# A decoder trunk on one core: the 16-row tail units of v, k and ckv computed in four column groups, the RMS scaling moved into the turning product, and the norm's weights moved into the split of w_in

## What is computed

```
u = rmsnorm(h, g_attn)             # h: (528, 1024), mean over 1024
proj = u @ w_in                    # w_in: (1024, 2216)
fq, fk, fv, ff, cq, ckv, kr = split(proj)   # 512, 512, 512, 8, 384, 256, 32 columns
rmsnorm(x, g) = x * rsqrt(mean(x * x) + 1e-6) * g
```

## Time and profile before

| | |
|---|---|
| median of 3 runs | 689.05 us (688.73 to 690.02) |
| the profiled execution | 692.33 us, of it 690.6 us in the profile's span |
| PE busy | 593.6 us, 86% of the span |
| DVE, ACT, POOL busy | 235.6, 207.3, 159.5 us |
| instructions | 8906 |
| input projection, first dense product to last | 27.8 to 157.2 us from the start of the span |

### The profile page before, as it was taken

The page is one execution under the profiler, slowest core; times in us unless marked ns, Lnnn a source line. Parts: engine busy times, 40 slices in busy tenths (PEclk is TensorE's granted clock), DMA queues, the critical chain, the costliest instruction groups (busy, mean ns, idle before and its releaser), DMA issues.

```text
span 690.6 us, 8906 instructions
## 1 busy us (share of the span) xinstructions
PE 593.6 (86%) x3367; PEld 382.0 (55%) x3367; DVE 235.6 (34%) x514; ACT 207.3 (30%) x377; POOL 159.5 (23%) x232
## 2 busy tenths in 40 slices
PE   3699999998999797999899976999998788887840
PEld 3598678895665454666455543555554455454520
DVE  4653323224456566364345540111111111011105
ACT  5533223242544343453344431121211111111110
POOL 8100001110134921242300021223232222122110
PEclk9999899999999999899999976999999999999985
DMA  8900000007600001000391076999999999999929
GB/s 246 387 28 1 1 0 1 1 1 228 284 1 0 0 1 62 0 1 1 135 416 58 32 254 216 375 382 394 382 387 394 397 398 393 393 395 394 389 97 354
DMA packets 35922, 136.01 MB, mean 197 GB/s; under 512 B 8920, under 2 KB 11016, under 8 KB 26928
## 3 DMA queue, kind: packets, MB, share of 16 engines
q1 hardware_dynamic: 29680, 124.92, 47.6%
q0 software_dynamic: 5632, 8.54, 3.9%
q10 hardware_dynamic: 576, 2.10, 0.7%
HBM read 131.28 MB, written 12.65 MB: 208 GB/s over the span
## 4 chain that ended last, share of the span: by engine, by line
PE 65%; SPq 12%; DMA 9%; DVE 8%; issue 4%; ACT 1%; POOL 0%; POOLq 0%; DVEq 0%
PE ps L1652 17%; PE ps L1927 10%; PE ps L1691 7%; PE ps L1782 6%; PE ps L1771 6%; PE ps L1954 5%; SPq L585 4%; DMA w<-in_w 4%; SPq L586 4%; SPq L592 4%; PE ps L1835 3%; DMA yg<-y_rows 2%; PE ps L1887 2%; PE ps L1747 2%; DMA xg<-u_rows,idx 1%
## 5 line engine op out<-in xcount | busy, mean ns | idle before, releaser
L1927 PE MATMUL ps<-w,xt 128*64 128x256 f32 x1024 | 127.8, 406 | 27.8 <-issue 22.3
L1927 PEld LDWEIGHTS ps<-w,xt 128*64 128x64 f32 x1024 | 84.4, 146 | 81.2 <-issue 52.0
L1522 DVE TENSOR_TENSOR xt<-ps,g_ffn_c 128x512 f32<-128x512 f32 x32 | 22.1, 692 | 212.6 <-PE ps L1887 212.6
L1954 PE MATMUL ps<-w,hT 128*64 128x512 f32 x256 | 61.8, 604 | 0.0
L799 POOL DMA_INDIRECT xg<-u_rows,idx x32 | 30.6, 957 | 125.7 <-PE ps L1887 106.3
L1081 ACT ACTIVATE hsb<-ps 128x256 f32<-128x256 f32 x32 | 12.3, 383 | 147.7 <-PE ps L1927 147.7
L789 POOL DMA_INDIRECT y_rows<-yh,idy x32 | 32.4, 1012 | 79.2 <-ACT yh L1099 79.2
L1691 PE MATMUL ps<-w_oa,mixT 128*128 128x512 f32 x96 | 45.9, 615 | 2.0 <-issue 2.0
L1782 PE MATMUL ps<-probT,vals 128*128 128x512 f32 (+4 forms) x160 | 42.6, 410 | 0.0
L1771 PE MATMUL ps<-qT,kT 68*128 68x400 f32 (+9 forms) x160 | 42.1, 407 | 0.0
L725 POOL TENSOR_SCALAR_AFFINE_SELECT probT<-probT 128x128 f32<-128x128 f32 (+2 forms) x80 | 20.2, 271 | 89.1 <-ACT probT L1004 88.6
(11 more groups left out here) (279 smaller groups left out, 906.1 us busy)
## 6 DMA issues: line engine op xcount, KB each, us to landing
w<-in_w SPq DMA_DIRECT2D x96, 1024.0 KB
yg<-y_rows SPq DMA_DIRECT2D x4, 1024.0 KB, 7.9
w_oa<-in_w_o SPq DMA_DIRECT2D x1, 3072.0 KB, 17.6
x<-in_x SPq DMA_DIRECT2D x4, 512.0 KB, 7.8
w_in_v<-in_w_in SPq DMA_DIRECT2D x1, 2048.0 KB, 11.2
w_in_k<-in_w_in SPq DMA_DIRECT2D x1, 2048.0 KB, 16.2
w_in_q<-in_w_in SPq DMA_DIRECT2D x1, 2048.0 KB, 20.0
u_rows<-u2n ACTq DMA_DIRECT2D x4, 512.0 KB, 4.3
```

The source lines that it names most:

```text
L1927: ins = pe.matmul(ps[j * slots:(j + 1) * slots, 2 + b, 0:F], xt[b][:, k, :], w13[s][:, j, k, :], start=(k == 0), stop=(k == DK - 1))
L1954: ins = pe.matmul(ps[q * slots:(q + 1) * slots, 6 + b, :], hT[b][:, m, :], w2s[s][:, m, q * 512:(q + 1) * 512], start=(m == 0), stop=(m == ...
```

## The change

- The turning product takes x itself as the stationary side and, as the moving side, a diagonal matrix `scale_x` with the inverse root on it. It is an ordinary fp32 product instead of a transpose, and `xs` is gone.
- `g_attn` is multiplied into the splits of `w_in`: ACT's copy to `w_hi` has it as its scale, and DVE's subtraction becomes a scalar_tensor_tensor. Since the weight of the norm is then one number for each partition and piece, the contraction is cut as `(k p)` instead of `(p k)`, the splits are made in eight pieces instead of two, and `g_attn` comes by POOL's queue ahead of the other small vectors, no longer by SP's. `u_full` is gone: ACT and DVE make `uT_hi` and `uT_lo` out of PSUM.
- The MT units of v, k and ckv are no longer projected. For each of them a `spread` of eight plain fp32 products goes behind the first, second and third unit of ffcq: piece k of the contraction goes to column group k mod 4, 32 rows of one bank, with `u_ends` (32 columns of u, times `g_attn`, made by DVE) as the stationary side and the `w_in` that is not yet split as the moving side. ACT copies the bank into `part`. In the place of the unit stands `gather`: one fp32 product with `groups`, a matrix of ones and zeros, which adds the four groups and puts the rows where the unit had them.

```
+SPREAD = ["v", "k", "ckv"]
+CG = P // 32
...
-        steps.append(("project", u))
+        steps.append(("gather" if in_groups(u) else "project", u))
         if n >= 1 and turned(units[n - 1]):
             steps.append(("turn", units[n - 1]))
+        if 1 <= n <= len(SPREAD):
+            steps.append(("spread", (SPREAD[n - 1], MT)))
...
-        xs = [place(f"xs{b}", [P, DK, P], F32, r_p + 4096 * b) for b in range(2)]
+        scale_x = [place(f"scale_x{b}", [P, P], F32, r_p + 6144 + 512 * b) for b in range(2)]
...
-        w_in_v = a["w_in"][0].rearrange("(p k) n -> p k n", k=DK)
+        w_in_v = a["w_in"][0].rearrange("(k p) n -> p k n", p=P)
...
-            sp.dma_start(g_attn[:, :], a["g_attn"][0].rearrange("(p k) -> p k", k=DK)).then_inc(consts_in, 16)
...
+                pool.dma_start(g_attn[:, :], a["g_attn"][0].rearrange("(k p) -> p k", p=P)).then_inc(consts_in, 16)
...
             def u_high(j):
-                c = key_cols(TOKEN_TILES[j])
-                act.wait_ge(turn_dve, j + 1)
-                act.activation(uT_hi[:, :, c], u_full[:, :, c], ACT.Copy).then_inc(u_hi_made, 1)
+                act.wait_ge(turned, j + 1)
+                act.activation(halves_x(uT_hi, j), turned_x(j), ACT.Copy).then_inc(u_hi_made, 1)
             def w_high(b):
                 act.wait_ge(win_in[b], 16)
+                if b == BLOCK_ORDER[0]:
+                    act.wait_ge(consts_in, 16)
...
-                for k0 in range(0, DK, DK // 2):
-                    act.activation(w_hi[b][:, k0:k0 + DK // 2, :], w_in[b][:, k0:k0 + DK // 2, :], ACT.Copy
+                for k in range(DK):
+                    act.activation(w_hi[b][:, k, :], w_in[b][:, k, :], ACT.Copy, scale=g_attn[:, k:k + 1]
                                    ).then_inc(w_hi_made, 1)
...
+                if j in (1, 2):
+                    u_high(j - 1)
+            u_high(2)
+            u_high(3)
+            u_high(4)
             w_high("ffcq")
-            u_high(len(TOKEN_TILES) - 1)
             w_high("v")
...
+            def copy_part(m):
+                b = SPREAD[m]
+                w = BLOCKS[b][1]
+                act.wait_ge(spread_done, m + 1)
+                act.activation(part[b][:, 0:w], ps[:, (m + 3) % 4, 0:w], ACT.Copy).then_inc(part_copied, 1)
...
             def u_low(j):
-                c = key_cols(TOKEN_TILES[j])
                 dve.wait_ge(u_hi_made, j + 1)
-                dve.tensor_tensor(uT_lo[:, :, c], u_full[:, :, c], uT_hi[:, :, c].bitcast(F32), ALU.subtract
+                dve.tensor_tensor(halves_x(uT_lo, j), turned_x(j), halves_x(uT_hi, j).bitcast(F32), ALU.subtract
                                   ).then_inc(u_lo_made, 1)
+            def u_end(j):
+                side, to, at, n = {0: (0, 0, 0, META), 1: (0, META, 0, 32 - META)}.get(j, (1, 0, P - 32, 32))
+                dve.wait_ge(u_hi_made, j + 1)
+                dve.tensor_tensor(
+                    u_ends[side][:, :, to:to + n].rearrange("p (q k) n -> p q k n", q=2), turned_x(j)[:, :, :, at:at + n],
+                    g_attn[:, :].rearrange("p (q k) -> p q k", q=2).unsqueeze(3).to_broadcast([P, 2, DK // 2, n]),
+                    ALU.mult).then_inc(ends_made, 1)
             def w_low(b, halves=(0, 1)):
-                for q in halves:
-                    k0 = q * DK // 2
-                    dve.wait_ge(w_hi_made, 2 * split_order.index(b) + q + 1)
-                    dve.tensor_tensor(w_lo[b][:, k0:k0 + DK // 2, :], w_in[b][:, k0:k0 + DK // 2, :],
-                                      w_hi[b][:, k0:k0 + DK // 2, :].bitcast(F32), ALU.subtract
-                                      ).then_inc(w_lo_made, 1)
+                if b in SPREAD:
+                    dve.wait_ge(spread_done, SPREAD.index(b) + 1)
+                for k in range(halves[0] * DK // 2, (halves[-1] + 1) * DK // 2):
+                    dve.wait_ge(w_hi_made, DK * split_order.index(b) + k + 1)
+                    dve.scalar_tensor_tensor(out=w_lo[b][:, k, :], in0=w_in[b][:, k, :], scalar=g_attn[:, k:k + 1],
+                                             in1=w_hi[b][:, k, :].bitcast(F32), op0=ALU.mult, op1=ALU.subtract
+                                             ).then_inc(w_lo_made, 1)
             def norm_tokens(j):
...
                 step(dve.reciprocal(rinv[j % 2][0:r, 0:1], root[0][0:r, j:j + 1]))
-                dve.tensor_scalar(xs[j % 2][0:r, :, :], src, rinv[j % 2][0:r, 0:1], None, ALU.mult
-                                  ).then_inc(xs_made, 1)
+                dve.tensor_scalar(scale_x[j % 2][0:r, 0:r], ident[0:r, 0:r], rinv[j % 2][0:r, 0:1], None, ALU.mult
+                                  ).then_inc(scale_made, 1)
+            dve.wait_ge(ident_made, 1)
+            dve.memset(groups[:, 0:P - 32], 0.0)
+            dve.tensor_reduce(groups[:, P - 32:], ident[:, :].rearrange("p (g c) -> p c g", g=CG), X, ALU.add
+                              ).then_inc(groups_made, 1)
             norm_tokens(0)
-            for j, t in enumerate(TOKEN_TILES):
-                r = rows(t)
+            for j in range(len(TOKEN_TILES)):
                 if j + 1 < len(TOKEN_TILES):
                     norm_tokens(j + 1)
-                if j == 0:
-                    dve.wait_ge(consts_in, 16)
-                dve.wait_ge(turned, j + 1)
-                for q in range(2):
-                    k0 = q * DK // 2
-                    ins = dve.tensor_tensor(
-                        u_full[:, k0:k0 + DK // 2, key_cols(t)],
-                        ps[:, 4 + 2 * (j % 2) + q, 0:DK // 2 * r].rearrange("p (k n) -> p k n", k=DK // 2),
-                        g_attn[:, k0:k0 + DK // 2].unsqueeze(2).to_broadcast([P, DK // 2, r]), ALU.mult)
-                ins.then_inc(turn_dve, 1)
-                if j >= 1:
-                    u_low(j - 1)
+                if j in (0, 1, len(TOKEN_TILES) - 1):
+                    if j == 0:
+                        dve.wait_ge(consts_in, 16)
+                    u_end(j)
+                u_low(j)
             w_low("ffcq")
-            u_low(len(TOKEN_TILES) - 1)
...
-                    pe.wait_ge(xs_made, j + 1)
+                    pe.wait_ge(scale_made, j + 1)
+                    src = xm[:, :] if t == MT else x[:, t, :]
                     for k in range(DK):
                         q, kk = divmod(k, DK // 2)
-                        ins = pe.transpose(ps[:, b0 + q, kk * r:(kk + 1) * r], xs[j % 2][0:r, k, :],
-                                           ident[0:r, 0:r])
+                        ins = pe.matmul(ps[:, b0 + q, kk * r:(kk + 1) * r], src[:, k * P:(k + 1) * P],
+                                        scale_x[j % 2][0:r, 0:r], start=True, stop=True)
...
+                if 3 <= n < 3 + len(SPREAD):
+                    pe.wait_ge(part_copied, n - 2)
+                done = DK * split_order.index(b)
                 for p, (ua, wa) in enumerate(((uT_hi, w_hi), (uT_lo, w_hi), (uT_hi, w_lo))):
                     for k in range(DK):
-                        if k % (DK // 2) == 0 and t == MT and p != 1:
-                            pe.wait_ge(w_lo_made if p else w_hi_made, done + k // (DK // 2) + 1)
-                        elif k == 0 and b == "q" and t == 0 and p != 1:
-                            pe.wait_ge(w_lo_made if p else w_hi_made, done + 2)
+                        if t == (MT if b == "ffcq" else 0) and p != 1:
+                            pe.wait_ge(w_lo_made if p else w_hi_made, done + k + 1)
...
+            def spread(b):
+                m = SPREAD.index(b)
+                w = BLOCKS[b][1]
+                pe.wait_ge(ends_made, 3)
+                pe.wait_ge(win_in[b], 16)
+                if m:
+                    unit_emptied(pe, m - 1)
+                for k in range(DK):
+                    g = k % CG
+                    ins = pe.matmul(ps[32 * g:32 * g + 32, (m + 3) % 4, 0:w], u_ends[0 if b == "k" else 1][:, k, :],
+                                    w_in[b][:, k, 0:w], start=k < CG, stop=k >= DK - CG)
+                ins.then_inc(spread_done, 1)
+            def gather(u):
+                n = unit_no[u]
+                b = u[0]
+                w = BLOCKS[b][1]
+                unit_emptied(pe, n - 4)
+                pe.wait_ge(groups_made, 1)
+                pe.wait_ge(part_copied, len(SPREAD) if n == 5 else SPREAD.index(b) + 1)
+                dst, side = ((ps[0:META, n % 4, 0:w], groups[:, P - 32:P - 32 + META]) if b == "k" else
+                             (ps[:, n % 4, 0:w], groups[:, :]))
+                pe.matmul(dst, side, part[b][:, 0:w], start=True, stop=True).then_inc(projected, 1)
```

More of the change, by code:

```diff
@@ L117, in unit_cols, with in_groups @@
     return block_cols(u[1]) if by_block(u) else key_cols(u[1])
+def in_groups(u):
+    return u[1] == MT and u[0] in SPREAD
 def projection_plan():
@@ L142, in build @@
     by_act = lambda u: u[0] in ("k", "q")
+    by_dve = lambda u: u[0] in ("ffcq", "ckv", "cum")
     staged = [u for u in turns if u[0] not in ("x", "cum")]
@@ L210, in build @@
```

(40 more changed lines are left out.)

7 lines of the change are left out of this document (3 added, 4 removed).

## The result

The changed kernel takes 0.9942 of the time of the kernel before (95% interval 0.9928 to 0.9956); the medians of 20 runs each are 687.35 us (684.52 to 690.49) against 691.46 (687.95 to 693.72). So it is faster, by 4.0 us (3.0 to 5.0), where 6.4 were forecast. The profiled execution took 685.2 us, 683.6 of them in the span: 7.0 less than the span before, more than the medians give. A single pair of profiles flatters the change by 3 us, and for the total only the ratio counts. The forecast of 682.6 us was counted down from the median of three runs, 689.05; the twenty runs of the same kernel have 691.46. So of the 4.75 us between 682.6 and 687.35, 2.4 come from the starting figure and 2.4 from the gain.

What follows compares the result with a forecast made beforehand. PE was taken to bound the kernel from 27.7 us on, DVE and ACT ahead of it. Removed units -9.85, spreads +4.5 and beginning -1.1 gave -6.4 us, from 689.05 to 682.6 us, range 680.5 to 688.0.

Steps and rivals of the forecast that it cites:

- I take 1.1 earlier: Start of the input projection, up to the first dense product: 1.1 us earlier, since the clock rises while x is turned.
- the term of 4.5 us for the spreads: Between ffcq units on PE: the three spreads cost 4.5 us together, with four column groups side by side.
- 0.9 later: Start of the projection: if the clock stays low, ffcq's low part ends at 28.6 us, 0.9 later than before.
- v: Place of the removed v MT unit: gain 3.9 us, with PE waiting for staging of the last ffcq unit.
- k: Place of the removed k MT unit: gain 4.7 us, with the low-clock loss of 2.56 us kept.
- The fit of 0.3 us: At k: staging of the MT rows is ready at 89.1 us, 0.3 ahead of k0's end at 89.4.
- ckv: Place of the removed ckv MT unit: gain 1.25 us, with PE waiting for staging of the last q unit.
- All of it reaches the end: Behind the projection: weight transfers are released by PE's steps, so all 6.4 us were expected to reach the end.
- The rival by which DMA swallows it: In the experts: they wait for DMA and the gain is lost, total 689 us; chance 4%.
- pairs: Rival, in the spreads: column groups overlap only two at a time, spreads 8.8 us, total 686.9 to 687.5; chance 12%.
- serial groups: Rival, in the spreads: the four groups run one after another, spreads 17.6 us, total 695.7, slower; chance 8%.
- The clock stays low in the turning products: Rival, at the start where x is turned: the clock stays low, +2.0 us, total 684.6; chance 10%.

Runs made afterwards that it cites:

- e5: Changed kernel with eight fp32 products of the identity with itself (results unused) on PE ahead of the first turning: 685.87 us, ratio 0.9924 to the kernel before.
- e9: Changed kernel with eight bf16 products of 512 columns of ones (results unused) on PE ahead of the first turning: 685.05 us, ratio 0.9906 to the kernel before.
- e1: Changed kernel without spreads and gathers, its three MT units projected as before, the rest of the change kept: 691.22 us, ratio 0.9998 to the kernel before.
- e3: Changed kernel with two column groups instead of four in the spreads: 691.95 us, ratio 0.9998 to the kernel before.
- e4: Changed kernel with all products of a spread in one column group: 703.0 us, ratio 1.014 to the kernel before.
- e2: Kernel before with only spreads and gathers added, its own scaling of x and splits in two pieces kept: 685.76 us, ratio 0.9914 to the kernel before.
- e11: e12 with e7's late turns besides: 682.08 us, ratio 0.9859 to the kernel before.
- e6: Changed kernel with bf16 filler products (results unused) between the small products of the ffcq MT unit: 686.47 us, ratio 0.9933 to the kernel before.
- e7: Changed kernel with the turn of the unit ahead of a gather moved behind the unit following it, for v and ckv: 686.54 us, ratio 0.9944 to the kernel before.
- e8: Changed kernel with the edits of e5, e6 and e7 at once: 684.92 us, ratio 0.9897 to the kernel before.
- e10: e2 with the fillers of e6 and the late turns of e7: 684.51 us, ratio 0.9882 to the kernel before.
- e12: Changed kernel with e9's start, e6's fillers and w_lo_q made behind the staging of the k MT rows: 683.67 us, ratio 0.9874 to the kernel before.

## Why the prediction was right in sign and too large

The step that failed is the term "I take 1.1 earlier" for the beginning, and beside it the term of 4.5 us for the spreads was too small. The runs showed 0.2 us later and 5.5 us in their places; together that is 2.3 of the 2.4 us by which 6.4 was too much. The three places of the missing units came out as forecast. The numbers of the kernel before, from its chain:

```profile
38.54 4.26 PE ps L1652 x24
...
43.13 4.29 PE ps L1652 x24
47.42 0.33 PE ps L1629 x3
...
53.64 22.25 PE ps L1652 x96
...
94.52 5.77 PE ps L1652 x24
...
143.91 3.19 PE ps L1652 x24
...
161.61 0.38 PE ps L1747
```

- **The beginning: this step failed.** "I take 1.1 earlier", 26.6 us for the first dense product, and it came at 27.9. Two things were wrong in it. The meta tile's turning was given no length of its own, and it took 3.56 us, nearly the 3.7 of a whole tile at that clock: its moving side has 16 columns instead of 128, but the records are as long. With the second tile behind it at 3.7, PE was not free for the third at 11.2, as forecast, but at 12.4. And behind it hangs a loop of three engines that I had followed through PE alone. ACT can't square the fourth tile before it has copied the second, which PE ends at 12.4; DVE makes the diagonal of the last tile (18.46) behind the low part of the third (17.13), so PE turns it at 18.9 to 20.9, where 19.3 was forecast as its end. That the clock rises on the way was right, as the 3.7 and 2.02 us for 16 equal records show; that work for PE from 1.7 us on would have raised it earlier is refuted by e5 and e9. The eight pieces of w_hi and w_lo took 4.19 and 4.38 us, forecast 3.7 and 4.4. The value of all this by e1 is nothing. The bound "0.9 later" stood in the text, and 0.2 later than before is what happened.
- **v:** forecast 3.9. From the end of the last ffcq unit to v0 the chain has 55.59 - 53.01 = 2.58 us; before it was 53.64 - 47.42 = 6.22. Gain 3.6.
- **k:** forecast 4.7, measured 5.0. From the end of the narrow cum products (81.84) to k's second unit (90.92) it is 9.08 us, where it was 14.08 (80.44 to 94.52); the low clock on k0 is there as taken over from the earlier trace rows. The fit of 0.3 us did not hold: w_lo_q started at 83.0 and not at 81.6, ended at 88.4, 1.4 later than forecast, and PE waited 0.41.
- **ckv:** forecast 1.25, measured 1.07 (138.97 to 143.91 before, 135.35 to 139.22 after).
- **The spreads:** forecast 4.5, measured 1.85 + 1.85 + 1.11 = 4.81. The choice between four and two groups was right, and e3 and e4 show what hung on it. A term was missing: each ffcq unit behind a spread takes 4.52 or 4.47 us, where one behind a turn took 4.26 to 4.29. That is 0.2 each and 0.7 in all; why was not tested. So the spreads cost 5.5.
- **The sum as it came out:** -3.6 - 5.0 - 1.1 + 5.5 + 0.2 = -4.0 at the end of the projection by these places. The chain enters attention at 156.91 instead of 161.61, 4.7 earlier. The other 0.7 is not from the places: from v0 to the end of the narrow cum products the two executions take 26.80 (before) and 26.25 us, and the first ffcq units differ by the rest. Of the forecast 6.4, 1.3 are missing in the beginning and 1.0 in the spreads; the places come to 9.7 where 9.85 was forecast.
- **All of it reaches the end:** right for the change itself, as far as can be told: 4.0 to 4.7 at the projection's end, 4.0 in the ratio. The rival by which DMA swallows it fell with e2 and e11. For a microsecond or two a single trace can't tell: in the fourteen traces, from the chain's entry into attention to the end of the span, code that no edit touches takes 524.0 us (e2) to 529.9 (e4 and e6), 529.0 before and 526.7 in the changed kernel, and it is not longer where attention begins earlier (528.0 in e11, which enters it first, at 152.43). So what e6 and e7 won in the chain (1.6 and 1.5 to 2.4 us) is less than this scatter, and neither ratio shows it, while the combinations that contain their edits have lower ratios (e8, e10, e11, e12). Why the clock and the time of the later stages differ between executions was not tested and stays open.
- **Rivals:** pairs and serial groups are refuted for this kernel by its own spreads of 1.85 us; e3 and e4 show what they would have cost. "The clock stays low in the turning products" is half right: it is low in xm's and in the second tile's, and that is part of the 1.3 us that are missing in the beginning.

## What to carry to other kernels

A unit of sixteen rows costs TensorE about as much as one of 128 (k's took 8.0 us at a mean clock of 0.65, a full one takes 5.57 at full clock); laid into four column groups side by side, in plain fp32 and with no splits, a unit of sixteen rows cost 1.85 + 0.86 + 0.2 = 2.9 us where the dense one cost 5.57. Part of that gain is taken again by the wait for staging that the unit had covered (0.9, 0.4 and 1.5 us here, against 14.3 us of units taken out), so read the waits at the place before you sum up products. Work taken from DVE or ACT at the start is worth something only if the loop it stands in is not held by another engine: follow all queues, with in-order waits, tile by tile. Where PE has only sparse products ahead of a dense part, filling the gap can keep the clock up (1.6 us in e6's chain, though its ratio doesn't show them). Judge a gain of a microsecond or two by many runs, since the later stages differed by up to 6 us between traces.

## What the runs showed of the hardware, unexpectedly

- Four column groups with four different moving sides lose 6% against the ideal: 6.98 us for one, 1.85 for four, 3.56 for two.
- The clock was low until about 13 us whether PE began at 5.1 us (the change), or at 1.7 with fp32 (e5) or bf16 products of full width (e9): in the last the second tile was still turned at 3.7 us for 16 records.
- At that clock 16 records of fp32 products with 16 moving columns took 3.56 us, and with 128 moving columns 3.7: an eighth of the columns saved nothing.
- The first dense unit after a stretch of sparse products (24 of 8 columns between 20.9 and 28.0 us, with 1.71 us as PE's longest idle time) began at a clock of 0.5 and took 6.1 to 7.4 us; with fillers ahead 4.6.
